# A hybrid block: decays' differences moved to ScalarE with one mask product on VectorE, and z's products with the norm's weights moved later on GpSimd

## The reference, cut to what matters

```python
    decay = jnp.exp(jnp.where(causal, g_cum[..., :, None] - g_cum[..., None, :], -jnp.inf))
    m = jnp.where(strict, jnp.einsum('bhnid,bhnjd->bhnij', k_beta, kc) * decay, 0.0)
...
    attn_intra = jnp.einsum('bhnid,bhnjd->bhnij', qc, kc) * decay
...
    o = o * lax.rsqrt(jnp.mean(o * o, axis=-1, keepdims=True) + EPS) * norm_w.astype(jnp.float32)
    o = o * jax.nn.silu(z.reshape(B, S, H, dh).astype(jnp.float32))
```

## Time and profile before

| | |
|---|---|
| median of 3 runs | 912.06 us (911.69 to 912.39) |
| the profiled execution, time | 912.35 us |
| the profiled execution, span | 910.5 us |
| busy: PE, DVE, ACT, POOL | 898.0, 602.7, 461.4, 90.9 us |
| weights' cast, ACT, line 1114 | 139 of 1.906 us |
| weights' subtraction, DVE, line 1582 | 139 of 2.309 us |
| granted TensorE clock, mean | 0.998 |

### The profile page before, as it was taken

One profiled execution on the slowest core, in us unless ns is written; L12 is line 12 of the kernel. 1 busy time (PEld: TensorE's weight loads), 2 busy tenths in 40 slices (PEclk: granted clock), 3 DMA queues, 4 the chain that ended last, 5 costly groups with the idle time before them and its releaser, 6 DMA issues.

```text
span 910.5 us, 12778 instructions
## 1 busy us (share of the span) xinstructions
PE 898.0 (99%) x5466; PEld 765.9 (84%) x5466; DVE 602.7 (66%) x705; ACT 461.4 (51%) x558; POOL 90.9 (10%) x92
## 2 busy tenths in 40 slices
PE   9999999999999999999999999999999999999997
PEld 8989888888888887888888878778788888888886
DVE  6889985777666557687867565555656666564665
ACT  7765554555444446645444255453355555454443
POOL 2142100100000000000125310110100000000000
PEclk9999999999999999999999999999999999999999
DMA  8734523244555554544565534454454356445531
GB/s 325 281 108 177 174 67 117 93 162 185 188 193 198 200 199 179 220 164 161 185 231 185 185 123 188 152 185 166 163 202 163 139 177 236 175 183 223 185 139 47
DMA packets 24218, 159.81 MB, mean 176 GB/s; under 512 B 3241, under 2 KB 3769, under 8 KB 5857
## 3 DMA queue, kind: packets, MB, share of 16 engines
q1 hardware_dynamic: 21600, 152.58, 45.8%
q0 software_dynamic: 2272, 6.24, 2.0%
q10 hardware_dynamic: 288, 0.17, 0.1%
HBM read 157.91 MB, written 2.63 MB: 176 GB/s over the span
## 4 chain that ended last, share of the span: by engine, by line
PE 80%; DVE 12%; ACT 4%; issue 2%; DMA 0%; POOL 0%; POOLq 0%; DVEq 0%; ACTq 0%
PE banks L494 31%; PE banks L462 20%; PE banks L465 10%; DVE t_wl L1582 4%; PE banks L434 4%; PE banks L585 3%; PE banks L522 2%; PE banks L739 2%; PE banks L993 2%; PE banks L405 1%; ACT t_wh L1114 1%; DVE t_hold L1600 1%; DVE t_xt L1600 1%; PE banks L943 1%; PE banks L1075 1%
## 5 line engine op out<-in xcount | busy, mean ns | idle before, releaser
L1582 DVE TENSOR_TENSOR t_wl<-t_raw,t_wh 128x2048 fp32r<-128x2048 f32 x139 | 318.0, 2309 | 123.2 <-ACT t_wh L1114 121.9
L462 PE MATMUL banks<-t_hx,t_wh 128*128 128x512 f32 x992 | 312.0, 396 | 0.0
L1114 ACT CAST t_wh<-t_raw 128x2048 fp32r<-128x2048 f32 x139 | 261.5, 1906 | 12.8 <-DMA t_raw<-in_W 8.1
L465 PEld LDWEIGHTS banks<-t_hx,t_wl 128*128 128x128 f32 x992 | 186.3, 188 | 43.8
L465 PE MATMUL banks<-t_hx,t_wl 128*128 128x256 f32 x992 | 194.9, 278 | 0.0
L462 PEld LDWEIGHTS banks<-t_hx,t_wh 128*128 128x128 f32 x992 | 153.3, 189 | 2.4
L494 PE MATMUL banks<-t_wh,t_hx 128*128 128x512 f32 x320 | 102.3, 396 | 0.0
L494 PEld LDWEIGHTS banks<-t_wh,t_hx 128*128 128x128 f32 x320 | 59.5, 188 | 12.7 <-issue 0.6
L494 PE MATMUL banks<-t_wl,t_hx 128*128 128x512 f32 x160 | 61.1, 390 | 0.0
L434 PE MATMUL banks<-t_hx,t_wh 128*128 128x256 f32 x336 | 60.6, 285 | 0.4 <-ACT t_hx L1157 0.4
L2187 POOL TENSOR_TENSOR t_st<-t_st,t_half 128x1 f32<-128x1 f32 (+1 forms) x18 | 10.6, 589 | 432.5 <-DVE t_st L1608 430.7
(11 more groups left out here) (310 smaller groups left out, 1265.5 us busy)
## 6 DMA issues: line engine op xcount, KB each, us to landing
t_raw<-in_W SPq DMA_DIRECT2D x143, 1024.0 KB, 4.8
skew<-scr POOLq DMA_DIRECT2D x1, 1536.0 KB, 16.3
t_x<-in_x SPq DMA_DIRECT2D x2, 512.0 KB, 4.8
t_tab<-in_tab POOLq DMA_DIRECT2D x1, 640.0 KB, 7.1
out<-t_xt SPq DMA_DIRECT2D x2, 320.0 KB, 2.3
t_raw<-in_W SPq DMA_DIRECT2D x1, 512.0 KB, 6.9
t_T<-skew POOLq DMA_DIRECT2D x4, 128.0 KB, 2.5
t_xt<-skew POOLq DMA_DIRECT2D x4, 128.0 KB, 2.4
```

Source lines behind the costliest of these rows:

```text
L462: e.matmul(bank[b + c], M.wh[:, h, wk], M.hx[:, k, :, :].rearrange("p a s -> p (a s)"), start=k == 0, stop=False)
L465: m = e.matmul(bank[b + c][:, 0:S], M.wl[:, h, wk], M.hh[:, k, :], start=False, stop=k == 7)
L1114: e.copy(M.wh[:, h, 0:n], M.raw[:, r, 0:n]).then_inc(q.sem, q.tick(("hi", i)))
L1582: e.tensor_tensor(M.wl[:, h, 0:n], M.raw[:, r, 0:n], M.wh[:, h, 0:n].bitcast(F32), ALU.subtract).then_inc(q.sem, q.tick(("lo", i)))
```

## The change

ACT now takes the differences: Relu of (g_cum of the row less the bank), with the sign turned by `scale=-1.0` and g_cum as the bias, 16 times 128x128 out of the banks; then it takes the exp of minus that. So where i > j there is exp(0) = 1 instead of 0, and DVE multiplies all of `dU` by the table `triu` (1 where i <= j). The Relus and the exp stand ahead of ACT's copy of conv unit 4; DVE's mask product stands behind its taps of unit 4. On POOL the two products of z with the norm's weights move from ahead of `kd` to behind all of `load_T`, where they wait for DVE's last mask product of the inverse, `("Ug", 2, 1)`. The table `cap` is loaded as before and no longer used.

```diff
-                        drain(b, DV, ("dU", g))
+                        drain(b, AC, ("drop", g))
...
             for u in range(6):
-                next_unit()
+                if u != 4:
+                    next_unit()
...
-                    if u == 5:
+                    if u == 3:
+                        next_unit()
+                        q.wait_ge(DV, "gc")
+                        for g in range(4):
+                            b = at["decay", g]
+                            q.wait_ge(PE, ("decay", g))
+                            for i in range(4):
+                                s = 4 * g + i
+                                e.activation(M.dU[:, s, :], bank[b][:, i * 128:i * 128 + 128], ACT.Relu, scale=-1.0,
+                                             bias=M.gcum[:, s:s + 1]).then_inc(q.sem, q.tick(("drop", g)))
+                        q.wait_ge(q, ("drop", 3))
+                        e.activation(M.dU[:], M.dU[:], ACT.Exp, scale=-1.0).then_inc(q.sem, q.tick("dexp"))
+                    elif u == 5:
                         silu_of(5)
...
-            q.wait_ge(DV, ("dU", 3))
-            e.activation(M.dU[:], M.dU[:], ACT.Exp).then_inc(q.sem, q.tick("dexp"))
...
-                elif u == 3:
-                    for g in range(4):
-                        b = at["decay", g]
-                        q.wait_ge(PE, ("decay", g))
-                        for i in range(4):
-                            s = 4 * g + i
-                            stt(M.dU[:, s, :], bank[b][:, i * 128:i * 128 + 128], M.gcum[:, s:s + 1], M.cap,
-                                ALU.subtract, ALU.min, ("dU", g))
+                elif u == 4:
+                    q.wait_ge(AC, "dexp")
+                    tt(M.dU[:], M.dU[:], rep(M.triu, 16), ALU.mult, "dU")
...
-            q.wait_ge(AC, "dexp")
+            q.wait_ge(q, "dU")
             tt(M.AT, M.dU[:], rep(M.nstrict, 16), ALU.mult, "dS")
...
-            for c in range(2):
-                z = heads(M.zz[:, c, :])
-                q.wait_ge(AC, ("zz", c))
-                q.wait_dma(LD["small"])
-                tt(z, z, rep(par("gdn_w"), 8), ALU.mult, ("zw", c))
             q.wait_ge(AC, ("kT", 1, 2))
             q.wait_ge(AC, "kdx")
             tt(heads(M.kd), heads(M.tm[:, 0, 512:1024]), bc(M.kdx[:, 0:8], 64), ALU.mult, "kd")
             q.wait_ge(DV, "ab_")
             for h in range(2, 8):
                 load_T(h)
+            q.wait_ge(DV, ("Ug", 2, 1))
+            for c in range(2):
+                z = heads(M.zz[:, c, :])
+                q.wait_ge(AC, ("zz", c))
+                q.wait_dma(LD["small"])
+                tt(z, z, rep(par("gdn_w"), 8), ALU.mult, ("zw", c))
```

More of the change, by code:

```diff
@@ L278, in memory @@
         M.kd = tm[:, 0, 0:512]
-        M.triu, M.nstrict, M.ones, M.near, M.same, delta, M.cap = (tab[:, i, :] for i in range(7))
+        M.triu, M.nstrict, M.ones, M.near, M.same, delta, _ = (tab[:, i, :] for i in range(7))
         M.delta = delta[:, 0:BASE]
```

## The result

| | before | after |
|---|---|---|
| median of 6 runs | 912.05 us (911.69 to 912.39) | 916.01 us (914.89 to 916.38) |
| profiled execution: time, span | 912.35, 910.5 us | 916.12, 914.3 us |
| busy PE, DVE, ACT, POOL | 898.0, 602.7, 461.4, 90.9 us | 898.7, 598.2, 468.0, 88.1 us |

The change makes the kernel slower: the ratio is 1.0042, with a 95% interval of 1.0029 to 1.0055. That is +3.96 us in the medians and +3.8 in the spans, where the forecast was +2.86. The busy times moved the way the change moves work (VectorE 4.5 us less, ScalarE 6.6 more, GpSimd 2.8 less); none of that says where the time went.

A forecast was written before the change was run, and what follows sets the result against it. TensorE, busy 898.0 of 910.5 us, bounds the kernel; ScalarE is without slack in the changed stretch. +3.21 (ScalarE's chain) - 0.35 (queries) = +2.86 us on 912.06 gives 914.9, range 913.6 to 916.1.

The forecast's parts named there:

- The Relus: Sixteen on ScalarE from 42.92, ahead of conv unit 4's copy: 0.26 us from start to start, last one ends at 47.18.
- The chain on ScalarE: Conv unit 4's copy 1.82 us late at 50.32, silu(3) starts at 53.15, work behind it 3.21 us late.
- rival C: ScalarE's table loads drain, 1.38 us each, two in the chain: +5.6 us in sum, 917.7 to 919.2; chance 0.04.
- The third load: Table load ahead of the attention's first exp, at 103.73: that exp 0.11 us late at most, counted as 0.
- The two new waits: TensorE waits 1.4 us for silu(3) near 52 and about 2.2 for silu(5), ending near 65.2: +3.21 us in all.
- The mask on VectorE: Mask multiply of 128x2048 on VectorE, 2.28 us, done before the reduction's squares at 59.6: cover 1.3 us, costs nothing.
- The relief for the queries: Moving z's products off GpSimd there speeds VectorE's nk(1) and kb(1); TensorE's wait at 75.35 goes: -0.35 us.
- Rival B: GpSimd's remaining products still slow VectorE's four, so the wait for the queries stays: +3.2 us, 915.3; chance 0.12.
- rival D: TensorE's clock falls in the new waits, a unit of 48 matmuls takes up to twice as long: +8.6, 920.7; chance 0.04.
- Later waits: From 120 us on, all TensorE waits as before.
- Rival E: Something off this chain, such as earlier weight loads, gives back 1 us or more: +1.5, 913.6; chance 0.05.
- rival A: Not slower: ScalarE's activations are cheaper than any row, Relus at 0.19 us or less each, bill under 1.8; chance 0.08.

The follow-up runs named there:

- z alone: The kernel before with only GpSimd's two products of z with the norm's weights moved behind the inverse: 911.50 us.
- first wait filled: The changed kernel with 10 idle transposes on TensorE in front of its first wait, for silu(3), the second wait left as it is: 915.87 us.

## Why the prediction was right, and where it fell short

The direction was right, and so was the mechanism of the larger part: ScalarE's hole is too short for the Relus, a load and the exp, and TensorE waits twice for it. The forecast of 914.9 was 1.1 us low. That 916.01 lies inside the range of 913.6 to 916.1 is luck: the fall of the clock, which the range left out, did happen, and the time stayed just under the upper edge only because its price was less than a third of what was feared and two other terms gave back 0.2 and 0.35 us. (By the prediction's own sum, 915.7 and 0.3, that edge is 916.0.)

- **The Relus**: 0.26 us from start to start were forecast, 4.22 us in all were measured, with the last end at 47.17 against 47.18. One Relu took 0.35 to 0.47 us, not 0.36 throughout. The nearest row by source, shape and pointer was the right one; the two bounds were not needed.
- **The chain on ScalarE**: copy at 50.32 forecast, 50.30 measured; silu(3) 53.15 and 53.12; silu(5)'s end 65.18 and 65.18.
- **The table load's drain** (rival C): it did not show, and the row was the right guide. The Trainium skill (ScalarE: Activation LUTs, What ACT_TABLE_LOAD costs) counts a drain of about 1380 ns for every switch besides the load, and the traces do not show it: in the changed kernel and with the exp between silu(4) and silu(5) each load starts within 0.02 us of the end of the instruction ahead, and the next one within 0.02 us of the load's end. The measurement decides.
- **The third load**, ahead of the attention's first exp: 0.11 us late at most were forecast. The exp starts at 108.13, 0.14 later than TensorE's delay of 4.26 explains, and no wait comes of it. Right.
- **The two new waits**: 1.4 and 2.2 forecast, 1.33 and 1.99 measured; TensorE 3.21 late, 3.20 measured.
- **The mask on VectorE**: 1.3 us of cover forecast, 1.26 left. Right.
- **The relief for the queries**: nk(1) and kb(1) at 0.65 forecast, 0.68 and 0.69 measured, and the wait goes. But the step "The wait of 0.35 at 75.35 goes: -0.35" took the idle time for the price, and z alone shows 0.55. And in the changed kernel the relief was not what removed the wait: with z's products in their old place it is gone too, because TensorE comes later. Rival B (the relief does not come) falls by the slowdown's own rows.
- **The clock** (rival D): this is the step that failed. It got a chance of 0.04 and a price of 5.8 us. It happened in the profiled execution and, by the mean clock, in five of six runs, at a price of 1.62 us. Two things in the step were off. I took the one fall in the trace, after 2.9 us without a matmul, as the measure of how long a wait must be, though nothing in it spoke of shorter ones; and I priced a whole unit at up to double, where the lower level lasted 3.4 us and doubled only what lay in it. Half of 3.4 us would have priced it at 1.7, an estimate. That it would come could not be read from the kernel before.
- **Later waits**: "from 120 us on all waits as before" was wrong by the one at 357.89, shorter by 0.34.

In the profile's own numbers the sum closes: 3.20 (ScalarE's chain) - 0.55 (queries) + 1.62 (clock) = 4.27, and 4.26 were measured at XT. Behind it come -0.35 at 357 and some 0.1 in other waits, which leaves the 3.8 of the spans. The relief of 0.55 stands in this sum because TensorE no longer waits for the queries, whichever way they come in time.

Rival E (a gain of 1 us or more elsewhere) and rival A (activations cheaper than any row) did not happen; what came back elsewhere was 0.35 us.

## What to carry to other kernels

An idle time of an engine off the critical path is room only up to its length, and table switches count in full: the 16 Relus alone fit the 5.49 us and cost nothing, while with the exp and one load ahead of the next copy, and a second load ahead of the silu, the chain came out 3.2 us late. Before moving a function to ScalarE, list the loads that its new neighbours force. And where TensorE is nearly always busy, price each new wait twice: by its idle time, and by the work behind it at the lower clock. Since the clock fell in some runs of a kernel and not in others, look at every run's mean clock before comparing medians of few runs.

## What the runs showed of the hardware that I had not expected

- The granted clock of TensorE falls after a wait of 1.99 us that ends before it falls, stays at the 1.2 GHz level for 3.4 us while TensorE is busy, and costs 1.62 us in the profile (1.2 to 1.7 between runs and kernels). It fell in five of six runs of the changed kernel and three of five with the first wait filled, in none of 11 with a single wait of 1.76 us at nearly the same place, and in none of nine with waits of 1.33 and 1.12 us. What decides between 1.76 and 1.99, or whether the place counts, stays open.
- Useless matmuls in a wait can pay: 16 transposes made the changed kernel 1.37 us faster, and 8 of them 1.44.
- A wait's price is more than its idle time: 0.35 shown, 0.55 lost. The first wait for silu(3) says the same: 1.33 us of idle time, and the matmuls behind it start at 54.44 instead of 52.85, 1.55 us later when the 0.04 by which this profile was late already are taken off.
- With 15 VectorE instructions more or fewer, a wait of TensorE 300 us later was 0.59 or 0.23 us long.
- Sixteen 128x128 activations out of PSUM with a bias pointer took ScalarE 4.22 us, one every 0.26 us; VectorE needed the same 4.22 us for its sixteen differences.
